# Expert passes of 112 slots instead of 128, with further passes that overlap

## The chip, the cores and the metric

The kernel runs on one core of a Trainium2 chip. The metric is the device time of one execution in microseconds (us); of several runs the median is taken. The core has five engines that work through their own instruction lists and wait for each other on semaphores: TensorE (PE, with its weight loads shown apart as PEld), VectorE (DVE), ScalarE (ACT), GpSimd (POOL) and SyncE (SP, which here only issues transfers).

## The reference

One decoder layer over 512 tokens of 1024 features in float32. The first sub-layer mixes tokens with two attention branches; the change does not touch it. The second is a mixture of 16 SwiGLU experts with a hidden width of 512:

```
logits = t @ router_w + router_b                      # t: 512 x 1024
probs  = softmax(logits)                              # 16 experts in 4 groups
g      = the group with the largest sum of its two best probabilities
experts, weights = the two best experts inside g, weights normalised
hidden = silu(t @ w_gate[e]) * (t @ w_up[e])          # for the experts chosen
y      = sum over the two experts of weight * (hidden @ w_down[e])
x      = x + gate2 * y
```

Each token goes to two experts, so an expert gets 64 tokens on average. Routed with the reference's inputs the fullest expert gets 103 and the emptiest 39.

## The kernel before, in words

The attention part and the router take the first 490 us or so. Then `expert_pass` runs over the 16 experts, each with a fixed number of slots for its tokens: 128, one per partition. If an expert has more tokens, `over` (L2010) is set, and each engine branches into further passes over all 16 experts for the tokens past the first 128. These passes are in the program but run only in that case.

Each engine has its own `stage` function that is called once per expert X, and `expert_pass` calls it for two experts at a time (b = 0 and b = 1). The order of the work is written out by hand in these functions:

- VectorE's `pick` (L2012) compares each token's position in its expert with a row 0 to 127 and writes `sel`, a bf16 table of 0 and 1, tokens by slots. It is done for two experts at once, in the stages with b = 0.
- TensorE's `slot_table` (L1082) multiplies `sel` (stationary, 128 x 128 bf16, four tiles of tokens and two experts, so eight matmuls) with `slot_t` (moving, four columns: token number and the weight in three bf16 parts). VectorE's `slot_index` (L2021) takes from it which token and which weight each slot has. An empty slot gets token 256 with weight 0.
- GpSimd's `fetch` (L619) gathers the slots' rows of 4 KB with an indirect transfer into `gx`; `scatter` (L611) adds the finished rows `ys` to the output with another.
- TensorE's `turn_rows` (L1071) turns the rows with eight transposes. ScalarE and VectorE split the result into a high and a low part, `hgT_hi` (L1509) and `hgT_lo` (L2052).
- The weights come from memory in chunks of 1 MB, six an expert. SyncE issues them up to twelve chunks ahead. ScalarE makes the high part `w_hi` (`high_e`, L1485) and VectorE the low part `w_lo` (`low_e`, L1928) of each chunk.
- `up_chunk` (L1102) and `down` (L1113) multiply with `three` (L660), three matmuls for each product of two split numbers. The slots are the stationary side, 128 x 128, and the weights the moving side, 512 columns. There are 48 such matmuls for gate and up and 24 for down in an expert.
- The hidden values are made by `silu` (L1522, L2073), turned by four transposes in `turn_hid` (L1149), and split into `hidT_hi` (L1538) and `hidT_lo` (L2092). The down product of expert X - 1 is done in the stage of expert X, between `turn_rows` and `turn_hid`.
- VectorE's `scaled` (L2034) multiplies the product with the slot's weight and a gate into `ys` (L2030).

TensorE's order in a stage, with `z` counting chunks:

```python
up_chunk(X, 0, b, z0, z)
pe.wait_ge(hg_sp, 2 * X + 2)
up_chunk(X, 1, b, z0, z + 1)
...
up_chunk(X, 2, b, z0, z + 2)
up_chunk(X, 3, b, z0, z + 3)
...
if b == 0 and more_:
    slot_table(X + 2, e + 2)
turn_rows(X + 1, 1 - b)
if not first_:
    down(X - 1, z0 + 4, z + 4)
turn_hid(X)
```

Buffers are single or double: four split chunks, twelve raw ones, two `gx`, one `ys`. The first two slot tables are made ahead of the first stage, in two groups of four matmuls; `keep_clock` (L728) puts idle matmuls around them. The last stage makes and uses `hidT` in two halves.

Of the kernel before, what the change touches and what calls it, by code (L numbers as in the profile page):

```python
# [20 lines left out]
F32R = mybir.dt.float32r  # L21
# [28 lines left out]
PASSES = S // P  # L50
# [30 lines left out]
def hybrid_layer(nc, x, c, w_ada, b_ada, norm1_g, w_in, q_norm_g, k_norm_g, rel_bias, w_o_a, w_o_b,  # L81
# [72 lines left out]
    hgT_hi = at("hgT_hi", [2, KD, P], F32R, 144)  # L154
    hgT_lo = at("hgT_lo", [2, KD, P], F32R, 152)
# [58 lines left out]
    with ExitStack() as ctx:  # L214
# [295 lines left out]
        def _(pool):  # L510
# [100 lines left out]
            def scatter(X):  # L611

                pool.wait_ge(y_sb, 2 * X + 2)
                if X:
                    pool.wait_ge(scat, 16 * X)
                pool.indirect_dma_start(out[0], bass.IndirectOffsetOnAxis(slot_tok[:, X % N_EXP:X % N_EXP + 1], 0),  # L616
                                        (ys_last if X % N_EXP == N_EXP - 1 else ys)[:, :], None, compute_op=ALU.add).then_inc(scat, 16)

            def fetch(X):  # L619

                pool.wait_ge(idx_ok, X + 1)
                if X >= 2:
# [33 lines left out]
        def _(pe):  # L656
# [414 lines left out]
            def turn_rows(X, b):  # L1071
# [4 lines left out]
                for u in range(2):  # L1076
                    for j in range(4):
                        kk = 4 * u + j
                        last = pe.transpose(ps[2 + u][:, P * j:P * j + P], gx[b][:, P * kk:P * kk + P], ident[:, :])
                    last.then_inc(hg_ps, 1)  # L1080

            def slot_table(X, e, singly=False):  # L1082
# [6 lines left out]
                for b in range(2):  # L1089
# [3 lines left out]
                    for tt in range(NT):  # L1093
                        last = pe.matmul(ps[7][:, 4 * b:4 * b + 4], sel[b][:, tt, :],
# [7 lines left out]
            def up_chunk(X, cc, b, z0, z):  # L1102
# [10 lines left out]
            def down(X, z0, z, halves=(0, 1)):  # L1113
# [16 lines left out]
            def down_last(X, z0, z, turn):  # L1130
# [4 lines left out]
                for n in range(2):  # L1135
                    for f in range(4):
# [5 lines left out]
                        m = three(ps[5 + n][:, :], (hidT_hi[:, f, :], hidT_lo[:, f, :]),  # L1142
# [65 lines left out]
        def _(act):  # L1208
# [297 lines left out]
            def hg_high(X, b):  # L1506
                for u in range(2):
                    act.wait_ge(hg_ps, 2 * X + u + 1)
                    act.activation(hgT_hi[:, b, 4 * u:4 * u + 4, :], ps[2 + u][:, :].rearrange("p (k s) -> p k s", k=4),  # L1509
                                   ACT.Copy).then_inc(hg_hi, 1)  # L1510

            def stage(X, Y, b, first_, last_):
# [9 lines left out]
                act.activation(silu[:, :], ps[0][:, :], ACT.Silu).then_inc(silu_ok, 1)  # L1522
# [7 lines left out]
                if last_:  # L1530
                    act.activation(hidT_hi[:, 0:2, :], ps[4][:, 0:2 * P].rearrange("p (k s) -> p k s", k=2), ACT.Copy
# [33 lines left out]
        def _(dve):  # L1565
# [444 lines left out]
            dve.tensor_scalar(over[:, :], over_f[:, :], P + 0.5, None, ALU.is_gt).then_inc(route_ok, 1)  # L2010

            def pick(X, e):  # L2012
# [3 lines left out]
                for b in range(2):  # L2016
                    dve.tensor_tensor(sel[b][:, :, :], iota[:, :].unsqueeze(1).broadcast_to([P, NT, P]),
                                      posm[:, :, bass.ds(e + b, 1)].broadcast_to([P, NT, P]), ALU.is_equal
                                      ).then_inc(sel_ready, 1)

            def slot_index(X, e, again, b):  # L2021
# [4 lines left out]
                dve.tensor_scalar(slot_tok[:, bass.ds(e + b, 1)], ps[7][:, 4 * b:4 * b + 1], float(S // 2), None, ALU.add)  # L2026
                dve.tensor_reduce(slot_w[:, bass.ds(e + b, 1)], ps[7][:, 4 * b + 1:4 * b + 4], AX.X, ALU.add).then_inc(idx_ok, 1)
# [122 lines left out]
```

## Time and profile before

| what | value |
|---|---|
| median of 3 runs | 819.32 us (815.22, 819.32, 819.73) |
| profiled execution: span from the first to the last instruction | 816.0 us |
| what lies around that span, if it is as long as the median run | 3.3 us |
| TensorE busy, of the span | 757.9 us (93%) |
| VectorE busy | 613.6 us (75%) |
| ScalarE busy | 430.4 us (53%) |
| GpSimd busy | 111.9 us (14%) |
| mean granted TensorE clock | 0.977 |

Times in the profile are microseconds from the start of the span. Matmuls are pipelined: a matmul's listed duration is longer than the distance to the next one, so TensorE's pace is read from the starts. A value in brackets after an instruction says how long its engine stood idle before it and which instruction ended that.

### The profile page before, as it was taken

The page shows a single profiled execution, that of the slowest core. Times are in us where ns is not written, and L with a number is a line of the kernel's source. Part 1 is how long each engine was busy: PE and PEld are TensorE (multiplying, and loading weights), DVE is VectorE, ACT ScalarE, POOL GpSimd, SP SyncE. Part 2 cuts the span into 40 slices and gives each one's busy share as a digit, 9 for nine tenths or more (in the row PEclk, how much of TensorE's full clock was granted, in tenths as well). Part 3 has the DMA queues.
Part 4 walks back from the last instruction along what each step waited for, and adds up shares of the span by engine and source line. Part 5 has one row for each costly group of instructions (what it writes and reads, how often), then busy time and mean ns, then how long its engine had stood idle before and what let it go on. Part 6 is the DMA issues. An engine that isn't in the chain of part 4 may idle for free.

```text
span 816.0 us, 9977 instructions
## 1 busy us (share of the span) xinstructions
PE 757.9 (93%) x3620; PEld 577.3 (71%) x3622; DVE 613.6 (75%) x803; ACT 430.4 (53%) x519; POOL 111.9 (14%) x90
## 2 busy tenths in 40 slices
PE   3899999999999898999999997999999999999992
PEld 3777777776665555667888874778888888788872
DVE  4676896623999958653566656799999999999991
ACT  6335124256665443555423442677767777767760
POOL 4020000000010100002000012013132232413111
PEclk9799999999999998999999999999999999999997
DMA  9928997110130131105438235999999999999973
GB/s 286 333 65 307 381 378 274 52 52 1 52 104 1 52 104 53 43 12 190 144 116 304 106 147 170 413 413 383 369 382 385 387 387 387 387 386 381 366 259 55
DMA packets 87307, 184.93 MB, mean 227 GB/s; under 512 B 8112, under 2 KB 27672, under 8 KB 85216
## 3 DMA queue, kind: packets, MB, share of 16 engines
q1 hardware_dynamic: 79200, 156.29, 51.2%
q0 software_dynamic: 8064, 28.09, 11.9%
q8 instruction: 24, 0.39, 0.2%
q14 instruction: 19, 0.16, 0.1%
HBM read 171.74 MB, written 12.62 MB: 226 GB/s over the span
## 4 chain that ended last, share of the span: by engine, by line
PE 51%; DVE 29%; issue 7%; ACT 5%; DMA 4%; SPq 1%; DVEq 1%; POOL 0%; ACTq 0%; POOLq 0%
PE ps L662 14%; PE ps L664 13%; PE ps L663 13%; DVE w_lo L1928 8%; DVE score L1750 3%; DVE ys L2030 3%; DVE m L1749 2%; ACT w_hi L1485 2%; DMA raw<-in_w_in 2%; DVE w_lo L1580 2%; PE ps L916 1%; PE ps L932 1%; DVE score L1736 1%; PE ps L944 1%; DVE sp L1701 1%
## 5 line engine op out<-in xcount | busy, mean ns | idle before, releaser
L1928 DVE TENSOR_TENSOR w_lo<-raw,w_hi 128x2048 fp32r<-128x2048 f32 x80 | 179.6, 2286 | 5.8 <-ACT w_hi L1485 5.8
L1485 ACT ACTIVATE w_hi<-raw 128x2048 fp32r<-128x2048 f32 x80 | 150.9, 1915 | 6.2 <-DMA raw<-in_w_gate 3.2
L662 PE MATMUL ps<-w_lo,hgT_hi 128*128 128x512 f32 x256 | 103.9, 406 | 4.3 <-DVE hgT_lo L2052 1.5
L662 PE MATMUL ps<-act_lo,w_hi 128*128 128x512 f32 x232 | 98.7, 426 | 5.3 <-issue 2.8
L663 PE MATMUL ps<-w_hi,hgT_lo 128*128 128x512 f32 x256 | 100.5, 393 | 0.0
L664 PE MATMUL ps<-w_hi,hgT_hi 128*128 128x512 f32 x256 | 100.5, 392 | 0.0
L664 PE MATMUL ps<-act_hi,w_hi 128*128 128x512 f32 x232 | 91.5, 395 | 0.0
L663 PE MATMUL ps<-act_hi,w_lo 128*128 128x512 f32 x232 | 91.4, 394 | 0.0
L1224 ACT ACTIVATE w_hi<-raw 128x2048 fp32r<-128x2048 f32 (+2 forms) x29 | 51.9, 1793 | 67.9 <-DMA raw<-in_w_in 44.9
L1580 DVE TENSOR_TENSOR w_lo<-raw,w_hi 128x2048 fp32r<-128x2048 f32 (+2 forms) x29 | 61.9, 2144 | 32.5 <-ACT w_hi L1224 32.3
L616 POOL DMA_INDIRECT out<-ys,slot_tok x15 | 48.8, 3255 | 159.2 <-DVE ys L2030 159.2
L662 PEld LDWEIGHTS ps<-act_lo,w_hi 128*128 128x128 f32 x232 | 44.0, 189 | 29.1 <-issue 14.6
L662 PEld LDWEIGHTS ps<-w_lo,hgT_hi 128*128 128x128 f32 x256 | 48.4, 189 | 20.5 <-DVE w_lo L1928 7.7
L664 PEld LDWEIGHTS ps<-w_hi,hgT_hi 128*128 128x128 f32 x256 | 48.5, 189 | 10.7
L663 PEld LDWEIGHTS ps<-w_hi,hgT_lo 128*128 128x128 f32 x256 | 48.6, 190 | 9.2
L662 PE MATMUL ps<-w_lo,act_hi 128*128 128x512 f32 x128 | 52.6, 411 | 1.3 <-DVE w_lo L1580 1.3
L662 PE MATMUL ps<-w_lo,hidT_hi 128*128 128x512 f32 x128 | 51.3, 401 | 2.1 <-issue 2.1
L664 PEld LDWEIGHTS ps<-act_hi,w_hi 128*128 128x128 f32 x232 | 44.0, 190 | 9.9
L664 PE MATMUL ps<-w_hi,act_hi 128*128 128x512 f32 x128 | 50.6, 395 | 0.0
L663 PE MATMUL ps<-w_hi,act_lo 128*128 128x512 f32 x128 | 50.5, 395 | 0.0
L664 PE MATMUL ps<-w_hi,hidT_hi 128*128 128x512 f32 x128 | 50.1, 391 | 0.0
L663 PE MATMUL ps<-w_hi,hidT_lo 128*128 128x512 f32 x128 | 49.9, 389 | 0.0
(279 smaller groups left out, 1378.1 us busy)
## 6 DMA issues: line engine op xcount, KB each, us to landing
raw<-in_w_down SPq DMA_DIRECT2D x32, 1024.0 KB, 16.9
raw<-in_w_gate SPq DMA_DIRECT2D x30, 1024.0 KB, 16.6
raw<-in_w_up SPq DMA_DIRECT2D x18, 1024.0 KB, 16.3
raw<-in_w_in SPq DMA_DIRECT2D x16, 1024.0 KB, 6.2
raw<-in_w_ada SPq DMA_DIRECT2D x16, 1024.0 KB, 7.3
raw_late<-in_w_up SPq DMA_DIRECT2D x14, 1024.0 KB, 19.0
raw<-in_w_ada SPq DMA_DIRECT2D x8, 512.0 KB, 6.6
raw_early<-in_w_ada SPq DMA_DIRECT2D x8, 512.0 KB, 5.5
```

The source lines that it names most:

```text
L616: pool.indirect_dma_start(out[0], bass.IndirectOffsetOnAxis(slot_tok[:, X % N_EXP:X % N_EXP + 1], 0), (ys_last if X % N_EXP == N_EXP - 1 e ...
L662: pe.matmul(o, a[0], b[1], start=start, stop=False)
L663: pe.matmul(o, a[1], b[0], start=False, stop=False)
L664: return pe.matmul(o, a[0], b[0], start=False, stop=stop)
L916: pe.matmul(zt[p % 2][:, r, 0:n], head(qbT, 2 * hp + r, P * i, P * i + P), kbT[DH * r:DH * r + DH, 0:n], start=True, stop=False, skip_grou ...
L1224: act.activation(cols(w_hi[spl_slot[w]], 0, top, nk), cols(raw[raw_slot[n]], 0, top, nk), ACT.Copy).then_inc(hi_ready, 1)
L1485: act.activation(e_hi[s_][:, :], e_raw[r][:, :], ACT.Copy).then_inc(e_top, 1)
L1580: dve.tensor_tensor(lo, r, hi.bitcast(F32), ALU.subtract).then_inc(chunk_split, 1)
L1749: link(dve.max(m8[r % 2][:, :], sc))
L1750: link(dve.match_replace(sc, m8[r % 2][:, :], sc, TAKEN))
L1928: dve.tensor_tensor(e_lo[s_][:, :], e_raw[r][:, :], e_hi[s_][:, :].bitcast(F32), ALU.subtract).then_inc(e_split, 1)
L2030: dve.scalar_tensor_tensor(out=dst[:, 512 * n:512 * n + 512], in0=ps[5 + n][:, :], scalar=slot_w[:, bass.ds(e, 1)], in1=gate2[:, 512 * n:5 ...
```

## The change

The number of slots becomes a constant, CAP = 112. All tiles with one column or row per slot shrink from 128 to 112, on the partitions or along the free dimension. The further passes become four (five passes in all), each shifted by 100 slots, so that two passes overlap by 12; the weights of tokens that an earlier pass has done are set to zero there.

```
-PASSES = S // P
+CAP = 112
+PASSES = -(-S // CAP)
+SHIFT = (S - CAP) // (PASSES - 1)
...
-    hgT_hi = at("hgT_hi", [2, KD, P], F32R, 144)
+    hgT_hi = at("hgT_hi", [2, KD, CAP], F32R, 144)
...
-    sel = [at(f"sel{i}", [NT, P], BF16, (200, 172)[i]) for i in range(2)]
+    sel = [at(f"sel{i}", [NT, CAP], BF16, (200, 172)[i]) for i in range(2)]
...
-    hidT_hi = at("hidT_hi", [4, P], F32R, 180)
+    hidT_hi = at("hidT_hi", [4, CAP], F32R, 180)
...
-                pool.indirect_dma_start(out[0], bass.IndirectOffsetOnAxis(slot_tok[:, X % N_EXP:X % N_EXP + 1], 0),
-                                        (ys_last if X % N_EXP == N_EXP - 1 else ys)[:, :], None, compute_op=ALU.add).then_inc(scat, 16)
+                pool.indirect_dma_start(out[0], bass.IndirectOffsetOnAxis(slot_tok[0:CAP, X % N_EXP:X % N_EXP + 1], 0),
+                                        (ys_last if X % N_EXP == N_EXP - 1 else ys)[0:CAP, :], None, compute_op=ALU.add).then_inc(scat, 16)
...
-                pool.indirect_dma_start(gx[X % 2][:, :], None, rows_d,
+                pool.indirect_dma_start(gx[X % 2][0:CAP, :], None, rows_d,
...
-                        last = pe.transpose(ps[2 + u][:, P * j:P * j + P], gx[b][:, P * kk:P * kk + P], ident[:, :])
+                        last = pe.transpose(ps[2 + u][:, CAP * j:CAP * j + CAP], gx[b][0:CAP, P * kk:P * kk + P],
+                                            ident[0:CAP, 0:CAP])
...
-                        last = pe.matmul(ps[7][:, 4 * b:4 * b + 4], sel[b][:, tt, :],
+                        last = pe.matmul(ps[7][0:CAP, 4 * b:4 * b + 4], sel[b][:, tt, :],
...
-                    m = three(ps[cc // 2][:, :], (hgT_hi[:, b, kk, :], hgT_lo[:, b, kk, :]),
+                    m = three(ps[cc // 2][0:CAP, :], (hgT_hi[:, b, kk, :], hgT_lo[:, b, kk, :]),
...
-                            m = three(ps[5 + n][:, :], (hidT_hi[:, f, :], hidT_lo[:, f, :]),
+                            m = three(ps[5 + n][0:CAP, :], (hidT_hi[:, f, :], hidT_lo[:, f, :]),
...
-                    t = pe.transpose(ps[4][:, P * f:P * f + P], silu[:, P * f:P * f + P], ident[:, :])
+                    t = pe.transpose(ps[4][:, CAP * f:CAP * f + CAP], silu[0:CAP, P * f:P * f + P], ident[0:CAP, 0:CAP])
...
-                act.activation(hidT_hi[:, :, :], ps[4][:, :].rearrange("p (k s) -> p k s", k=4), ACT.Copy
+                act.activation(hidT_hi[:, :, :], ps[4][:, 0:4 * CAP].rearrange("p (k s) -> p k s", k=4), ACT.Copy
...
-            dve.tensor_scalar(over[:, :], over_f[:, :], P + 0.5, None, ALU.is_gt).then_inc(route_ok, 1)
+            dve.tensor_scalar(over[:, :], over_f[:, :], CAP + 0.5, None, ALU.is_gt).then_inc(route_ok, 1)
...
-                    dve.tensor_tensor(sel[b][:, :, :], iota[:, :].unsqueeze(1).broadcast_to([P, NT, P]),
-                                      posm[:, :, bass.ds(e + b, 1)].broadcast_to([P, NT, P]), ALU.is_equal
+                    dve.tensor_tensor(sel[b][:, :, :], iota[:, 0:CAP].unsqueeze(1).broadcast_to([P, NT, CAP]),
+                                      posm[:, :, bass.ds(e + b, 1)].broadcast_to([P, NT, CAP]), ALU.is_equal
...
-                dve.scalar_tensor_tensor(out=dst[:, 512 * n:512 * n + 512], in0=ps[5 + n][:, :],
-                                         scalar=slot_w[:, bass.ds(e, 1)], in1=gate2[:, 512 * n:512 * n + 512],
+                dve.scalar_tensor_tensor(out=dst[0:CAP, 512 * n:512 * n + 512], in0=ps[5 + n][0:CAP, :],
+                                         scalar=slot_w[0:CAP, bass.ds(e, 1)], in1=gate2[0:CAP, 512 * n:512 * n + 512],
...
-                    dve.tensor_tensor(hgT_lo[:, b, 4 * u:4 * u + 4, :], ps[2 + u][:, :].rearrange("p (k s) -> p k s", k=4),
+                    dve.tensor_tensor(hgT_lo[:, b, 4 * u:4 * u + 4, :], ps[2 + u][:, 0:4 * CAP].rearrange("p (k s) -> p k s", k=4),
...
-                dve.tensor_tensor(silu[:, :], ps[1][:, :], silu[:, :], ALU.mult).then_inc(hid_ok, 1)
+                dve.tensor_tensor(silu[0:CAP, :], ps[1][0:CAP, :], silu[0:CAP, :], ALU.mult).then_inc(hid_ok, 1)
...
-                    dve.tensor_scalar(posm[:, :, :], posm[:, :, :], float(-P), None, ALU.add).then_inc(posm_ok, 1)
-                    dve.wait_ge(posm_ok, p)
+                    dve.tensor_scalar(posm[:, :, :], posm[:, :, :], float(-SHIFT), None, ALU.add).then_inc(posm_ok, 1)
+                    dve.wait_ge(posm_ok, p * 2 - 1)
+                    for n in range(1, 4):
+                        last = dve.scalar_tensor_tensor(out=slot_t[:, :, :, n], in0=posm[:, :, :], scalar=CAP - SHIFT - 0.5,
+                                                        in1=slot_t[:, :, :, n], op0=ALU.is_ge, op1=ALU.mult)
+                    last.then_inc(posm_ok, 1)
+                    dve.wait_ge(posm_ok, p * 2)
```

Left out are the same edit for hgT_lo, hidT_lo, slot_tok, slot_w, ScalarE's hgT_hi and silu, the last down product and the halves of hidT in the last stage.

## Rows read from the trace of the kernel before

**Rows 1.** Stages: start:end, length, busy us of each engine, clock, DMA share, GB/s.

```profile
500.00:520.00 20.00, 15.67 (x77) 12.49 (x76) 10.73 (x13) 7.79 (x9) 1.78 (x3) 0.91 0.91 327
640.00:680.00 40.00, 39.75 (x197) 32.33 (x196) 38.89 (x32) 27.79 (x23) 11.31 (x5) 1.00 1.05 387
```

**Rows 2.** Chain that ended last, in order of time: start, us, what.

```profile
639.33 0.50 PE ps L662
...
657.48 0.50 PE ps L662
...
675.92 0.50 PE ps L662
...
712.50 0.50 PE ps L662
```

**Rows 3.** Timeline of all engines, 640 to 661: start, us, instruction, idle before.

```profile
649.18 0.60 ACT L1538 ACTIVATE hidT_hi<-ps 128x512 fp32r<-128x512 f32 x1 [3.47 <-PE ps L1153]
...
651.52 0.39 PE L664 MATMUL ps<-w_hi,hgT_hi 128*128 128x512 f32 x1
...
651.61 2.29 DVE L1928 TENSOR_TENSOR w_lo<-raw_late,w_hi 128x2048 fp32r<-128x2048 f32 x1 [1.11 <-ACT w_hi L1485]
...
656.97 0.39 PE L664 MATMUL ps<-w_hi,hgT_hi 128*128 128x512 f32 x1
...
660.37 0.27 PEld L1094 LDWEIGHTS ps<-slot_t,sel 128*128 128x128 bf16 x8 [0.27 <-issue]
...
660.57 0.86 PEld L1079 LDWEIGHTS ps<-ident,gx 128*128 128x128 f32 x8
```

**Rows 4.** Timeline of all engines, 667 to 672.

```profile
667.61 0.60 ACT L1538 ACTIVATE hidT_hi<-ps 128x512 fp32r<-128x512 f32 x1 [3.46 <-PE ps L1153]
...
668.11 5.51 ACT L1485 ACTIVATE w_hi<-raw 128x2048 fp32r<-128x2048 f32 x3
...
669.41 0.69 DVE L2092 TENSOR_TENSOR hidT_lo<-ps,hidT_hi 128x512 fp32r<-128x512 f32 x1
...
670.05 2.29 DVE L1928 TENSOR_TENSOR w_lo<-raw,w_hi 128x2048 fp32r<-128x2048 f32 x1
```

**Rows 5.** Weight loads by form, whole span: count, then busy us, mean ns, idle.

```profile
L663 PEld LDWEIGHTS ps<-w_hi,hgT_lo 128*128 128x128 f32 x256 | 48.6, 190 | 9.2
...
L1079 PEld LDWEIGHTS ps<-ident,gx 128*128 128x128 f32 x128 | 14.3, 140 | 4.8 <-DMA gx<-rows_scratch,slot_tok 3.8
...
L944 PEld LDWEIGHTS ps<-pT,vb 128*64 128x64 f32 x80 | 5.1, 140 | 5.0 <-issue 3.3
...
L1094 PEld LDWEIGHTS ps<-slot_t,sel 128*128 128x128 bf16 x64 | 2.2, 96 | 4.6 <-DVE sel L2017 2.7 <-issue 1.8
```

**Rows 6.** Timeline of TensorE, 330 to 385: matmuls of 512 columns in bf16.

```profile
347.30 0.38 PE L922 MATMUL ps<-masks,identb 128*128 128x512 bf16 x1 [0.16 <-issue]
353.74 0.61 PE L922 MATMUL ps<-masks,identb 128*128 128x512 bf16 x2
...
366.06 0.60 PE L922 MATMUL ps<-masks,identb 128*128 128x512 bf16 x2
```

**Rows 7.** VectorE and ScalarE by form, 490 to 816.

```profile
L2092 DVE TENSOR_TENSOR hidT_lo<-ps,hidT_hi 128x512 fp32r<-128x512 f32 x15 | 10.3, 689 | 0.5 <-ACT hidT_hi L1538 0.5
L2017 DVE TENSOR_TENSOR sel<-iota,posm 128x512 bf16<-128x512 f32 x16 | 10.3, 686 | 0.0
...
L2082 DVE TENSOR_TENSOR hidT_lo<-ps,hidT_hi 128x256 fp32r<-128x256 f32 x1 | 0.4, 420 | 0.0
...
L1538 ACT ACTIVATE hidT_hi<-ps 128x512 fp32r<-128x512 f32 x15 | 9.0, 599 | 48.0 <-PE ps L1153 48.0
...
L1531 ACT ACTIVATE hidT_hi<-ps 128x256 fp32r<-128x256 f32 x1 | 0.4, 385 | 0.5 <-PE ps L1153 0.5
```

**Rows 8.** GpSimd's DMA queue, 497 to 504 (gathers) and 796 to 816 (scatters).

```profile
q0 software_dynamic: 231, 0.86, 39.7%
...
q0 software_dynamic: 288, 1.05, 34.2%
```

**Rows 9.** ScalarE's weight parts, by form and first wait for a transfer.

```profile
L1485 ACT ACTIVATE w_hi<-raw 128x2048 fp32r<-128x2048 f32 x80 | 150.9, 1915 | 6.2 <-DMA raw<-in_w_gate 3.2 <-DMA raw<-in_w_down 2.6 <-PE ps L664 0.2
...
713.16 1.92 ACT L1485 ACTIVATE w_hi<-raw 128x2048 fp32r<-128x2048 f32 x1 [0.66 <-DMA raw<-in_w_gate]
```

More of the change, by code:

```diff
@@ L153, in hybrid_layer @@
     lbias = at("lbias", [N_EXP], F32, 173.65625)
-    hgT_hi = at("hgT_hi", [2, KD, P], F32R, 144)
-    hgT_lo = at("hgT_lo", [2, KD, P], F32R, 152)
+    hgT_hi = at("hgT_hi", [2, KD, CAP], F32R, 144)
+    hgT_lo = at("hgT_lo", [2, KD, CAP], F32R, 152)
     amp2r = at("amp2r", [D], F32, 160)
@@ L161, in hybrid_layer @@
     gx = [at(f"gx{i}", [D], F32, 164 + 4 * i) for i in range(2)]
-    sel = [at(f"sel{i}", [NT, P], BF16, (200, 172)[i]) for i in range(2)]
+    sel = [at(f"sel{i}", [NT, CAP], BF16, (200, 172)[i]) for i in range(2)]
     silu = at("silu", [F_EXP], F32, 178)
-    hidT_hi = at("hidT_hi", [4, P], F32R, 180)
-    hidT_lo = at("hidT_lo", [4, P], F32R, 198)
+    hidT_hi = at("hidT_hi", [4, CAP], F32R, 180)
+    hidT_lo = at("hidT_lo", [4, CAP], F32R, 198)
     gate2 = at("gate2", [D], F32, 174)
@@ L1141, in down_last @@
                             pe.wait_ge(hidT_sp2, turn)
-                        m = three(ps[5 + n][:, :], (hidT_hi[:, f, :], hidT_lo[:, f, :]),
+                        m = three(ps[5 + n][0:CAP, :], (hidT_hi[:, f, :], hidT_lo[:, f, :]),
                                   (e_hi[s_][:, a:a + 512], e_lo[s_][:, a:a + 512]), f == 0, f == 3)
@@ L1508, in hg_high @@
                     act.wait_ge(hg_ps, 2 * X + u + 1)
-                    act.activation(hgT_hi[:, b, 4 * u:4 * u + 4, :], ps[2 + u][:, :].rearrange("p (k s) -> p k s", k=4),
+                    act.activation(hgT_hi[:, b, 4 * u:4 * u + 4, :], ps[2 + u][:, 0:4 * CAP].rearrange("p (k s) -> p k s", k=4),
                                    ACT.Copy).then_inc(hg_hi, 1)
@@ L1521, in stage @@
                     act.wait_ge(hidT_ps, X)
-                act.activation(silu[:, :], ps[0][:, :], ACT.Silu).then_inc(silu_ok, 1)
+                act.activation(silu[0:CAP, :], ps[0][0:CAP, :], ACT.Silu).then_inc(silu_ok, 1)
                 if not first_:
@@ L1530, in stage @@
                 if last_:
-                    act.activation(hidT_hi[:, 0:2, :], ps[4][:, 0:2 * P].rearrange("p (k s) -> p k s", k=2), ACT.Copy
+                    act.activation(hidT_hi[:, 0:2, :], ps[4][:, 0:2 * CAP].rearrange("p (k s) -> p k s", k=2), ACT.Copy
                                    ).then_inc(hidT_h, 1)
@@ L1534, in stage @@
                     act.wait_ge(hidT_sp, X + 1)
-                    act.activation(hidT_hi[:, 2:4, :], ps[4][:, 2 * P:4 * P].rearrange("p (k s) -> p k s", k=2), ACT.Copy
+                    act.activation(hidT_hi[:, 2:4, :], ps[4][:, 2 * CAP:4 * CAP].rearrange("p (k s) -> p k s", k=2), ACT.Copy
                                    ).then_inc(hidT_h2, 1)
                     return
-                act.activation(hidT_hi[:, :, :], ps[4][:, :].rearrange("p (k s) -> p k s", k=4), ACT.Copy
+                act.activation(hidT_hi[:, :, :], ps[4][:, 0:4 * CAP].rearrange("p (k s) -> p k s", k=4), ACT.Copy
                                ).then_inc(hidT_h, 1)
@@ L2081, in stage @@
                     dve.wait_ge(hidT_h, X + 1)
-                    dve.tensor_tensor(hidT_lo[:, 0:2, :], ps[4][:, 0:2 * P].rearrange("p (k s) -> p k s", k=2),
+                    dve.tensor_tensor(hidT_lo[:, 0:2, :], ps[4][:, 0:2 * CAP].rearrange("p (k s) -> p k s", k=2),
                                       hidT_hi[:, 0:2, :].bitcast(F32), ALU.subtract).then_inc(hidT_sp, 1)
@@ L2086, in stage @@
                     dve.wait_ge(hidT_h2, last_)
-                    dve.tensor_tensor(hidT_lo[:, 2:4, :], ps[4][:, 2 * P:4 * P].rearrange("p (k s) -> p k s", k=2),
+                    dve.tensor_tensor(hidT_lo[:, 2:4, :], ps[4][:, 2 * CAP:4 * CAP].rearrange("p (k s) -> p k s", k=2),
                                       hidT_hi[:, 2:4, :].bitcast(F32), ALU.subtract).then_inc(hidT_sp2, 1)
@@ L2091, in stage @@
                 dve.wait_ge(hidT_h, X + 1)
-                dve.tensor_tensor(hidT_lo[:, :, :], ps[4][:, :].rearrange("p (k s) -> p k s", k=4),
+                dve.tensor_tensor(hidT_lo[:, :, :], ps[4][:, 0:4 * CAP].rearrange("p (k s) -> p k s", k=4),
                                   hidT_hi[:, :, :].bitcast(F32), ALU.subtract).then_inc(hidT_sp, 1)
```

6 lines of the change are left out of this document (3 added, 3 removed).

## The prediction

> **What bounds the kernel now.** The change touches only the experts, the last 326 us or so, so I read that stretch alone. The table of stages shows the matrix engine and VectorE both nearly full in it: of 40 us PE is busy 39.75 and DVE 38.89, at full clock [rows 1]. Busy shares do not say which of the two sets the pace, so the chain of waits comes next. It repeats every two experts: a matmul that waits for a weight part opens at 639.33, 657.48, 675.92, 712.50 [rows 2]. A half without a slot table (639.33 to 657.48) takes 18.15 us, a half with one (657.48 to 675.92) 18.44, the pair 36.59; 675.92 to 712.50 is the same again.
>
> The timeline shows one loop in both halves. PE runs 12 matmuls, eight transposes of gathered rows, 24 down matmuls and four hidden transposes. ScalarE sits idle for 3.47 us until those transposes end, turns them (hidT_hi at 649.18), and only then makes the next w_hi, for which VectorE waits 1.11 us (651.61) [rows 3]. Two w_lo parts with ys between them follow, and the second releases PE at 657.48. From hidT_hi to that release it is 8.3 us. In the other half the same steps stand at 667.61, 668.11 and 670.05, and 668.11 plus one w_hi of 1.92 is 670.03: again the ACT step releases VectorE, though VectorE has only just ended hidT_lo (669.41 plus 0.69) [rows 4]. So what counts is what lies in PE's part of the loop (about 9.8 us, 10.1 with a slot table), hidT_hi, w_hi, two w_lo and ys. Other VectorE work counts only once it is late.
>
> **The change, part by part.**
>
> *Further passes.* The fullest expert holds 103 tokens (worked out by routing the reference's inputs). 103 is under 112 as it is under 128, the branch is not taken, and the new code in it (three multiplies a pass, a fifth pass) costs nothing. Were it taken, four more passes of some 300 us each would stand in the time.
>
> *The matmuls of the experts.* The moving side stays 512 wide; the slots are the stationary side, whose load shrinks from 128 to 112 columns. Loads get cheaper by the column: 128 columns take 190 ns, 64 take 140 [rows 5], 0.78 ns a column, so 112 should show some 177. But PE does not wait for a load: 24 steps from 651.52 to 656.97 give a pitch of 0.227 us [rows 3], of which 512 columns at 2.4 GHz are 0.213, and the load lies under it. What the other 0.014 us is, decides. If it is a fixed price of changing weights, 112 columns save nothing; if it follows the columns, an eighth of it, 1.7 ns; if the load's whole shortening came back, 13 ns. In the loop are 36 matmuls an expert, so 16 experts give 0, 1.0 or 7.7 us. The nearest row is a bf16 pair of 512 columns: alone 0.38, as a pair 0.60 to 0.61, a pitch of 0.22 to 0.23 [rows 6], though its loads take half as long (rows below). A load half as long leaves the pitch as it was, so I take a fixed price: 0. The range keeps 7.7.
>
> *The slot table's loads.* This is the part against the change. These matmuls take sel as bf16 stationary, and sel goes from 128 to 112 columns. I take the slow way at 112 columns, 0.103 x 112 / 128 = 0.090, because nothing in the rows shows the fast way for anything but 128 columns. A table of eight then costs 8 x (0.090 - 0.025) = 0.52 us more. PE works in order, and behind the table wait the row transposes, the down matmuls and the hidden transposes, hence ScalarE, VectorE and the end of the half: it is inside the loop. There are 64 such loads [rows 5]: the opening two groups of four, one table in the first stage, six in the steady halves. Seven tables are 3.6 us; of the opening 0.52 I count 0.4, the first group running beside the second sel. Sum +4.0.
>
> The Trainium skill, page "TensorE: Matmul & The Clock Gate", section "Weight-path perf modes — Fast Weight Load (FWL) and DoubleRow", has this as a rule: the fast load is on only when the number of weights is 128 and the type is not FP32. The trace agrees for full loads (bf16 fast, f32 slow); no row shows a narrower bf16 load. By that rule the sum below stands; without it, it is 4.0 lower. The section "LDWEIGHTS (loading the stationary operand)" there puts a load at columns / 1.2, by which I estimate 93 ns for 112 columns, much as the slow slope does.
>
> *Evictions and picks by the slot.* hidT, hgT and sel have 448 elements a partition instead of 512. hidT_lo takes 689 ns for 512 and 420 for 256, so 64 fewer save 0.067; hidT_hi 599 and 385, so 0.053; sel (686) counts as hidT_lo [rows 7]. In the loop only hidT_hi is on the path: 16 x 0.053 = 0.85. In the run-up two sel, three hgT_hi and one hgT_lo give 0.35. The rest falls into VectorE's slack and is worth nothing unless PE gets faster. If VectorE's tie at 670.05 were binding, it would give up to 0.33 a pair, but the later slot table takes its place. Sum -1.2. silu and ys lose partitions, not elements: 0, for want of a row that shows a gain.
>
> *Rows fetched and scattered.* Sixteen of 128 descriptors fall away. On the path are the first gather (PE has nothing before it) and the last scatter. Two scatters keep the DMA engines busy 34.2% of 20 us, 3.4 us each; gathers 39.7% of 7 us for 231 packets, 1.5 us per 128 [rows 8]. An eighth of each: 0.43 and 0.19. The issue of the first gather may shrink too, or not: 0 to 0.3. Taken: -0.6. The 14 gathers and 15 scatters between are hidden.
>
> *Transposes.* Their stationary side stays 128 columns (the model dimension); rows and moving columns become 112. The load sets their pitch: 0. Bound above: a rival.
>
> **Sum.** +4.0 - 1.2 - 0.6 + 0 = +2.2 us on the profiled span of 816.0, so 818.2. The median of the runs, 819.32, lies 3.3 above that span; I keep this difference: 821.5 us. The three runs are 4.5 us apart, so under 0.5% (4.1 us) cannot be told from no change.
>
> **Rivals.** *The fast bf16 load survives 112 columns.* Then -1.8, 817.5 us. For it: the load is still most of the array. Against it: no row. Chance 0.25.
>
> *The weight load does space the stream.* The 0.014 us falls with the columns: by an eighth, 820.5; altogether, 813.8, and PE leaves the loop's 9.8 us by 0.48 a half. For it: all f32r rows pay it. Against it: the bf16 pair. Chance 0.08 for the eighth, 0.07 for all.
>
> *Slower: the f32 transposes lose their short load.* They load 140 ns where plain f32 takes 190 [rows 5]. If 112 rows bar them from that, each of 12 an expert costs 50 ns more, 0.6 us a half inside PE's part, 9.6 in all: 831. It decides from 20 ns a transpose on, beside the tables. Against it: columns, not rows, set load times in the trace. Chance 0.05. Also on this side: the clock. Between 500 and 520 the mean granted clock was 0.91 [rows 1], so part of that stretch ran at 1.2 GHz, 0.09 x 20 = 1.8 us lost, after PE had idled for the first rows; slower opening tables shift that, and a second such stretch would bring 823.3.
>
> *The transfers set the pace.* ScalarE waits for weights from 713.16 on, 5.8 us in all [rows 9]; fewer row descriptors would take that away: down to 815.7. Against it: the pair's length is the same before the first wait (639.33 to 675.92) and at 675.92 to 712.50, and ScalarE has idle time each half. Chance 0.08.
>
> *The change does not do what it says* (further passes run): 0.01.
>
> **Chances and range.** The forecast has 0.46. It ends slower by over 0.5% in 0.10 of that, the transposes and the clock add 0.09, unforeseen waits 0.03: slower 0.22. Faster: the whole of the pitch 0.07, transfers 0.05, a part of the surviving fast load 0.05, the rest 0.02: 0.19. Within 0.5%: 0.59. The range runs from the transfers' case with a little more, 815.0, to the forecast with a second slow-clock stretch and a dearer load (0.103), 825.0; left out are the whole pitch below and the transposes above.
>
> **What would show it.** Right: the slot table's loads at some 170 ns instead of 96, about 0.09 apart; f32r pitch still 0.227; hidT_hi near 546 ns; the pair near 37.0 us, its half with the table longer by 0.47 and the other shorter by 0.05. Wrong: loads at 96 (the pair 36.5), a pitch near 0.215, transposes' loads at 190, or ScalarE's waits for weights gone together with a shorter pair.

## The result and the profile after

| what | before | after |
|---|---|---|
| median of 4 runs each, on one chip | 819.53 us | 826.99 us (825.03 to 829.73) |
| ratio after to before, 95% interval | | 1.0124 [1.0093, 1.0155] |
| profiled execution: span | 816.0 us | 822.9 us (its run: 825.03 us) |
| first to fifteenth scatter | 250.86 us | 261.82 us |

The change costs 1.2%. The prediction was 821.5 us with a range up to 825.0, so it was too low. Times of kernels with the fault found below spread by up to 2%: runs more than 1.5% above the fastest of their kernel are left out of the ratios, and three of their profiles (e6, e7, f2) are of such long executions.

The page of after says where to look. GpSimd was busy for 111.9 us before; now the scatter alone takes 144.4, and the chain that ended last lies for a quarter of the span on the scatter's transfer (DMA 4% of it before).

```profile
PE 759.5 (92%) x3622; PEld 560.5 (68%) x3622; DVE 611.2 (74%) x803; ACT 428.3 (52%) x519; POOL 202.3 (25%) x90
...
DMA out<-ys,slot_tok 25%; PE ps L664 10%; PE ps L666 9%; PE ps L665 9%; DVE score L1753 3%; DVE m L1752 3%; DMA raw<-in_w_ada 2%; DVE w_lo L1583 2%; DVE ys L2033 1%; PE ps L918 1%; DVE score L1739 1%; DVE sp L1704 1%; PE ps L934 1%; DVE w_lo L1931 1%; DVE accm L1642 1%
...
L618 POOL DMA_INDIRECT out<-ys,slot_tok x15 | 144.4, 9627 | 121.9 <-DVE ys L2033 121.9
```

By stages, what [rows 1] showed is less full: PE and DVE lost some 2.4 and 1.5 us of 40, GpSimd more than doubled. (The clock from 500 to 520 is 1.00 here.)

```profile
500.00:520.00 20.00, 17.34 (x90) 13.05 (x91) 13.81 (x17) 12.06 (x12) 1.84 (x2) 1.00 0.98 364
640.00:680.00 40.00, 37.33 (x180) 27.98 (x179) 37.42 (x32) 27.48 (x22) 26.09 (x5) 1.00 1.04 367
```

The chain over one pair answers to [rows 2]. It no longer goes through PE: scatter, landing, ys, scatter.

```profile
638.76 0.75 DVE ys L2033
639.51 0.27 issue
639.78 16.48 DMA out<-ys,slot_tok
...
658.07 17.65 DMA out<-ys,slot_tok
...
676.51 0.75 DVE ys L2033
677.26 0.27 issue
677.53 16.54 DMA out<-ys,slot_tok
```

There is one buffer ys, so `scaled` (L2037) waits until the scatter before it has landed. Landing 16.48, then 1.81 to the next scatter (two halves of ys 1.41, the gaps before and behind them 0.40) make 18.29, the distance from 639.78 to 658.07; 17.65 + 1.81 = 19.46, the distance to 677.53. That is the pair of 37.75 us, 36.59 before. Before, the scatter at 637.35 landed after 10.9 us, and the next ys began at 653.82, 16.5 us after its start: 5.6 us to spare.

The timeline of VectorE and GpSimd in the same half shows why the landing is late. The scatter begins 0.36 us into the first of four w_lo and ends 1.47 us after silu begins. The last scatter, with VectorE idle, takes 1.47 us in all.

```profile
639.42 8.89 DVE L1931 TENSOR_TENSOR w_lo<-raw,w_hi 128x2048 fp32r<-128x2048 f32 x4
639.78 9.91 POOL L618 DMA_INDIRECT out<-ys,slot_tok  x1 [5.48 <-DVE ys L2033]
648.22 0.68 DVE L2076 TENSOR_TENSOR silu<-ps,silu 112x512 f32<-112x512 f32 x1
...
811.32 1.47 POOL L618 DMA_INDIRECT out<-ys_last,slot_tok  x1 [6.78 <-DVE ys_last L2033]
```

The lines of the kernel before in such a half:

```profile
636.99 8.89 DVE L1928 TENSOR_TENSOR w_lo<-raw,w_hi 128x2048 fp32r<-128x2048 f32 x4
637.35 3.39 POOL L616 DMA_INDIRECT out<-ys,slot_tok  x1 [3.57 <-DVE ys L2030]
...
653.82 1.40 DVE L2030 SCALAR_TENSOR_TENSOR ys<-ps,slot_w,gate 128x512 f32<-128x512 f32 x2
```

A scatter's length and end are what the profile gives; that it waits first and works in its last 1.47 us is read from these ends. So GpSimd waits for 8.4 us, through w_lo after w_lo (two inputs from SBUF each), and works when silu (one input from PSUM) begins. Before, the same scatter took 3.4 us: it ended 1.5 us after the first boundary between two w_lo (639.19), and ran beside the second w_lo without making it longer. Both start 0.36 us after their w_lo does. What changed is that it no longer gets in at a boundary.

The Trainium skill, page "SBUF — State Buffer", section "Who interferes with whom", says that VectorE and GpSimd share one pair of SBUF ports as a lock and that a VectorE instruction with two SBUF inputs contends with a GpSimd instruction that reads SBUF. The long waits agree; the scatters before, which ran beside a w_lo, do not fit a plain lock.

The rows that answer to [rows 5], [rows 7] and [rows 9], by form (ScalarE waits for weights 1.2 us at most now, being held up itself):

```profile
L665 PEld LDWEIGHTS ps<-w_hi,hgT_lo 128*112 128x112 f32 x256 | 45.1, 176 | 13.3
L1081 PEld LDWEIGHTS ps<-ident,gx 112*128 112x128 f32 x128 | 13.6, 144 | 3.8 <-DMA gx<-rows_scratch,slot_tok 2.5 <-issue 0.2
L1097 PEld LDWEIGHTS ps<-slot_t,sel 128*112 128x112 bf16 x64 | 4.5, 131 | 3.4 <-DVE sel L2020 2.3
...
L1541 ACT ACTIVATE hidT_hi<-ps 128x448 fp32r<-128x448 f32 x15 | 8.2, 545 | 49.6 <-PE ps L1156 49.6
...
L1488 ACT ACTIVATE w_hi<-raw 128x2048 fp32r<-128x2048 f32 x79 | 149.5, 1914 | 2.8 <-PE ps L666 1.6
...
L2033 DVE SCALAR_TENSOR_TENSOR ys<-ps,slot_w,gate 112x512 f32<-112x512 f32 x30 | 21.1, 746 | 8.9 <-DMA out<-ys,slot_tok 7.1 <-PE ps L666 1.8
```

### The profile page after: what moved, and what is told of

Its sections match the earlier page's. It is cut to its first block, busy times and chain, and to the rows that moved or that the text cites. A ratio compares the mean times of both kernels' runs of the same rounds, so it can differ in the third digit from the quotient of the medians.

```text
span 822.9 us, 9979 instructions
## 1 busy us (share of the span) xinstructions
PE 759.5 (92%) x3622; PEld 560.5 (68%) x3622; DVE 611.2 (74%) x803; ACT 428.3 (52%) x519; POOL 202.3 (25%) x90
## 3 DMA queue, kind: packets, MB, share of 16 engines
q0 software_dynamic: 7552, 25.99, 11.5%
## 4 chain that ended last, share of the span: by engine, by line
PE 39%; DMA 29%; DVE 19%; issue 7%; ACT 4%; SPq 1%; POOL 1%; DVEq 0%; POOLq 0%; ACTq 0%
DMA out<-ys,slot_tok 25%; PE ps L664 10%; PE ps L666 9%; PE ps L665 9%; DVE score L1753 3%; DVE m L1752 3%; DMA raw<-in_w_ada 2%; DVE w_lo L1583 2%; DVE ys L2033 1%; PE ps L918 1%; DVE score L1739 1%; DVE sp L1704 1%; PE ps L934 1%; DVE w_lo L1931 1%; DVE accm L1642 1%
## 5 line engine op out<-in xcount | busy, mean ns | idle before, releaser
L618 POOL DMA_INDIRECT out<-ys,slot_tok x15 | 144.4, 9627 | 121.9 <-DVE ys L2033 121.9
L664 PE MATMUL ps<-w_lo,hgT_hi 128*112 128x512 f32 x256 | 103.9, 406 | 11.3 <-DVE w_lo L1931 9.8
L666 PE MATMUL ps<-w_hi,hgT_hi 128*112 128x512 f32 x256 | 101.9, 398 | 0.0
L665 PE MATMUL ps<-w_hi,hgT_lo 128*112 128x512 f32 x256 | 100.9, 394 | 0.0
L664 PEld LDWEIGHTS ps<-w_lo,hgT_hi 128*112 128x112 f32 x256 | 44.8, 175 | 31.0 <-DVE w_lo L1931 14.9
L666 PEld LDWEIGHTS ps<-w_hi,hgT_hi 128*112 128x112 f32 x256 | 44.8, 175 | 14.8
L664 PE MATMUL ps<-w_lo,hidT_hi 128*112 128x512 f32 x128 | 52.1, 407 | 2.6 <-issue 2.6
L665 PEld LDWEIGHTS ps<-w_hi,hgT_lo 128*112 128x112 f32 x256 | 45.1, 176 | 13.3
L666 PE MATMUL ps<-w_hi,hidT_hi 128*112 128x512 f32 x128 | 51.3, 401 | 0.0
L665 PE MATMUL ps<-w_hi,hidT_lo 128*112 128x512 f32 x128 | 50.8, 397 | 0.0
```

The costliest lines, as they stand in the source:

```text
L664: pe.matmul(o, a[0], b[1], start=start, stop=False)
L665: pe.matmul(o, a[1], b[0], start=False, stop=False)
L666: return pe.matmul(o, a[0], b[0], start=False, stop=stop)
```

## The experiments

In each, "issue" is the time of one scatter on GpSimd (median of 15), and the ratio is to the kernel before on the same chip.

**First: is it the 112-row scatter?** e1 is the kernel before with this alone, e4 the same with 96; e2 is the changed kernel with sel, slot table, index, ys and scatter back at 128; e3 the changed kernel with one more instruction in each stage.

```diff
-  ...slot_tok[:, X % N_EXP:...], (ys_last if ... else ys)[:, :]
+  ...slot_tok[0:112, X % N_EXP:...], (ys_last if ... else ys)[0:112, :]      # e1; 0:96 in e4
```

```diff
                 low_e(z + 3, z0 + 3)
+                if not first_ and not second_:                                # e3
+                    dve.tensor_copy(qkg[:, 0:64], ps[7][:, 64:128])
```

> The kernel before, in which the scatter alone takes 112 rows (slots 112 to 127, all empty here, are not added); slot tables, picks, gathers, transposes, matmuls and evictions keep 128 slots. Theory (the loss is the scatter's: with 112 rows its issue on GpSimd no longer gets in between two of VectorE's instructions, and ys waits for it): GpSimd's scatter lengthens from 3.3 us to 9 to 10 us in the mean, its landing from 10.9 to some 16.5 us, VectorE's ys waits 5 to 7 us in all for it, pairs of 37.5 us or more instead of 36.6, time 5 to 8 us over the kernel before (824 to 828). Rival (the loss sits in TensorE's part, from the slower loads of the slot table and the f32r pitch of 0.231): scatter still 3.3 us, time within 1.5 us of the kernel before.

> The kernel before, in which the scatter alone takes 96 rows; the tokens of slots 96 and up (seven, all of the one fullest expert) are not added to the output. Theory A (any number of rows that is not 128 makes the issue miss the gap between two VectorE instructions): issue 9 us or more, time as with 112 rows, 824 to 828. Theory B (a multiple of 32 rows still gets in): issue 2.7 to 3.4 us, time that of the kernel before or 1 us less. Rival (the loss is not the scatter's at all): issue 3.3 us or a little less, no change.

> The changed kernel with sel, the slot table, its index and weight, ys and the scatter back at 128 slots; the gather, the transposes, silu, hgT, hidT and all f32r matmuls stay at 112. Theory (scatter): the scatter's issue falls back to 3.3 to 3.6 us, its landing to some 11 us, ys waits for nothing but TensorE; time 818 to 821, that is, the kernel before's less the shorter evictions (0.85) or with the longer pitch (0.003 us x 36 x 16 = 1.7) added. Rival (TensorE's part): what is left in it, the f32r pitch of 0.231, carries most of the loss, and the time stays at 823 or more. Read beside it: the f32r pitch at 112 stationary columns, 0.231 again if the columns set it, 0.228 if it came with the scatter.

> The changed kernel with one more VectorE instruction in each steady stage: a copy of 64 columns from PSUM into a spare SBUF buffer (a dead value) after the second of the low parts w_lo, so that VectorE's run of subtractions that read two SBUF inputs is broken by an instruction that reads none. Theory (the 112-row scatter waits on GpSimd through the whole run of such subtractions and starts when it ends): the scatter's issue drops from 9.6 us to 5 or less, the wait of ys shrinks to under 2 us in all, and 4 to 7 us come back (819 to 823). Rival (112 rows take GpSimd longer to work through, whatever VectorE does): the issue stays at 9 to 10 us and the time is that of the changed kernel or longer by the copies, 827 to 829.

| run | ratio | issue, us | landing, us |
|---|---|---|---|
| e1 | 0.9989 [0.9969, 1.0010] | 3.29 | 10.4 |
| e4 | 0.9971 [0.9947, 0.9995] | 3.25 | 9.5 |
| e2 | 1.0029 [1.0012, 1.0046] | 3.36 | 10.4 |
| e3 | 0.9980 [0.9959, 1.0002] | 3.30 | 10.3 |

The row count is not the cause: my first theory fell (e1 and e4 came out as its rivals had it). That it is the scatter stands: e3 takes the whole loss back with 14 copies of 0.22 us, and in its timeline the scatter gets in at the copy (635.62 + 1.47 = 637.09, its end).

```profile
633.42 2.28 DVE L1931 TENSOR_TENSOR w_lo<-raw,w_hi 128x2048 fp32r<-128x2048 f32 x1
635.62 0.22 DVE L2066 COPY qkg<-ps 128x64 f32<-128x64 f32 x1
635.76 6.68 DVE L1931 TENSOR_TENSOR w_lo<-raw,w_hi 128x2048 fp32r<-128x2048 f32 x3
...
633.78 3.31 POOL L618 DMA_INDIRECT out<-ys,slot_tok  x1 [3.79 <-DVE ys L2033]
```

**Second: which of the narrowed parts?** e5 is the changed kernel with ys on 128 partitions; e6 the kernel before with ys and scatter at 112; e7 the changed kernel with pick, table and index at 128; e8 the kernel before with all narrowed but the f32r matmuls, their transposes, evictions and silu.

```diff
-  dve.scalar_tensor_tensor(out=dst[0:CAP, ...], in0=ps[5 + n][0:CAP, :],      # e5; the reverse in e6
-                           scalar=slot_w[0:CAP, ...], in1=gate2[0:CAP, ...],
+  dve.scalar_tensor_tensor(out=dst[:, ...], in0=ps[5 + n][:, :],
+                           scalar=slot_w[:, ...], in1=gate2[:, ...],
```

> The changed kernel with ys alone written on all 128 partitions again (the slot weights past 112 are zero); pick, slot table, index, gather, scatter and matmuls stay at 112. The runs so far say that neither the scatter's 112 rows alone nor the gathers, transposes and f32r matmuls of 112 starve the scatter; left are ys on 112 partitions and the pick with its slot table, alone or together with the scatter. Theory Y (ys on 112 partitions is needed): scatter's issue 3.3 us, time 815 to 819. Rival T (the narrower pick and slot table do it): issue 9 to 10 us as in the changed kernel, time 825 to 829.

> The kernel before with ys and the scatter at 112 partitions and rows, all else at 128 (slots 112 to 127 are empty). Theory Y (ys on 112 partitions, read by a scatter of 112 rows, is enough by itself): issue 9 us or more, time 823 to 828. Rival T: issue 3.3 us, time that of the kernel before, 816 to 820.

> The changed kernel with sel, the slot table's matmuls, the token index and the weight back at 128 slots; gather, matmuls, ys and scatter stay at 112. Theory T (the narrower pick is needed for the starving): issue 3.3 us, time 815 to 820, and pairs of some 36.3 us, 0.2 shorter than in the run with the copy, whose tables are still slow. Theory Y: issue 9 to 10 us, time 823 to 828.

> The kernel before with pick, slot table, index, gather, ys and scatter at 112, and the f32r matmuls, their transposes and evictions and silu at 128: the changed kernel without the smaller stationary side. If the stationary side has no part in the starving (theories Y and T alike): issue 9 to 10 us, time 824 to 829. Rival (the starving needs the changed timing of TensorE or ScalarE too): issue 3.3 us, time 817 to 821, the longer slot tables (0.17 us each) in it.

| run | ratio | issue, us | landing, us |
|---|---|---|---|
| e5 | 1.0006 [0.9983, 1.0028] | 3.30 | 10.3 |
| e6 | 1.0174 [1.0089, 1.0258] | 9.92 | 17.0 |
| e7 | 1.0096 [1.0066, 1.0125] | 9.91 | 17.1 |
| e8 | 1.0150 [1.0078, 1.0222] | 9.91 | 17.1 |

Theory Y holds in all four for the issue; the times of e6 and e8 (833.6 and 832.8 us) lie above what was expected. e1 and e6 differ only in the partition count of ys, an instruction that takes the same 0.74 us and ends the same 0.28 us before the scatter; the issue goes from 3.29 to 9.92 us.

```profile
L616 POOL DMA_INDIRECT out<-ys,slot_tok x15: 1462/3292/3337, 545.5 to 796.5; - x15
```

```profile
L616 POOL DMA_INDIRECT out<-ys,slot_tok x15: 1462/9915/11147, 547.0 to 819.2; - x15
```

(The scatter's line in e1, then in e6: ns, minimum, median and maximum.)

**Third: ys itself, the last instruction, or any partial one?** A copy of 64 elements stands behind ys: full in the changed kernel (e9), on 112 partitions in the kernel before (e10), full in the kernel before (f1). In f3 the copy on 112 stands in front of ys. e11 has ys and scatter at 96, f2 only the first half of ys at 112.

```diff
+  dve.tensor_copy(qkg[0:112, 0:64], ps[7][0:112, 64:128])                     # f3
   scaled(X - 2, e - 2, b)
+  dve.tensor_copy(qkg[:, 0:64], ps[7][:, 64:128])                             # e9, f1; 0:112 in e10
```

```diff
+  rows = 112 if n == 0 else P                                                 # f2
+  dve.scalar_tensor_tensor(out=dst[0:rows, ...], in0=ps[5 + n][0:rows, :], ...
```

> The changed kernel (ys on 112 partitions) with a copy of 128 partitions x 64 elements from PSUM into a spare SBUF buffer directly behind ys, so that it has ended before the scatter starts; the run of w_lo behind it is unbroken. Theory L (what counts is the partition count of VectorE's last instruction before the run of full ones): scatter's issue 3.1 to 3.4 us, time 815 to 820. Rival D (what counts is that the rows of ys itself were written on 112 partitions): issue 9 to 11 us, time 823 or more.

> The kernel before (ys and scatter at 128) with a copy of 112 partitions x 64 elements from PSUM into a spare SBUF buffer directly behind ys. Theory L (the last instruction before the run): the 128-row scatter starves too, issue 9 to 11 us, time 823 or more. Rival D (ys itself): issue 3.1 to 3.4 us, time 816 to 820.

> The kernel before with ys and scatter at 96 partitions and rows (the seven tokens of the fullest expert in slots 96 and up are not added to the output). Theory P (anything less than 128 partitions starves the scatter): issue 9 to 11 us, time 823 or more. Rival Q (only a number that is no multiple of 32 does, and 96 does not): issue 3.1 to 3.4 us, time 815 to 819.

> The kernel before with a full copy (128 partitions x 64 elements, PSUM to a spare SBUF buffer) directly behind ys: the control of the run with the copy on 112 partitions. Theory S (a VectorE instruction on fewer than 128 partitions shortly before the run makes the scatter miss its boundaries, and a full one does not undo it): with no partial instruction there the issue stays at 3.1 to 3.5 us and the time at 817 to 821, the copies' 0.13 us a half in it. Rival M (it is the extra 0.13 us, which moves the boundary from 1.84 to 1.97 us behind the scatter's start, or the copy as such): issue 9 to 11 us, time 830 or more.

> The kernel before with the scatter at 112 rows and only the first of the two instructions of ys on 112 partitions, the second on 128; nothing added, so every boundary stays where it was. Theory S (a partial instruction shortly before, not undone by a full one behind it): issue 9 to 11 us, time 823 or more. Rival L (only the last instruction before the run counts): issue 3.3 us, time 816 to 820.

> The kernel before with the copy on 112 partitions x 64 elements placed in front of the two full instructions of ys instead of behind them. Theory S: the scatter starves as it does with the copy behind ys, issue 9 to 11 us, time 823 or more. Rival L (only the last instruction before the run counts): issue 3.3 us, time 817 to 821.

| run | partial instruction | ratio | issue, us |
|---|---|---|---|
| e9 | ys, then a full copy | 1.0178 [1.0135, 1.0220] | 10.04 |
| e10 | copy behind a full ys | 1.0338 [1.0296, 1.0381] | 10.13 |
| e11 | ys at 96 | 1.0145 [1.0103, 1.0187] | 9.87 |
| f1 | none | 1.0023 [0.9997, 1.0049] | 3.51 |
| f2 | first half of ys | 1.0183 [1.0111, 1.0255] | 9.92 |
| f3 | copy in front of a full ys | 1.0316 [1.0276, 1.0357] | 3.4 and 11.2 in turn |

e9 and e10 each refuted one of their two theories: it is neither the last instruction alone (e9) nor ys (e10, where a scatter of all 128 rows starves). f1 clears the copy. What is common to all starved kernels is a VectorE instruction on fewer than 128 partitions shortly before the run, and a full one behind it does not undo that. 96 is no better than 112; one scatter of e11, the fourteenth, was worse and let silu (one input from PSUM) pass as well:

```profile
792.24 12.97 POOL L616 DMA_INDIRECT out<-ys,slot_tok  x1 [8.29 <-DVE ys L2030]
```

f3 came out as neither of its theories had it, and shows the exception. Where copy and ys follow each other the scatter starves; where VectorE stood idle for 1.85 us between them, it does not:

```profile
604.41 0.22 DVE L2060 COPY qkg<-ps 112x64 f32<-112x64 f32 x1
606.48 1.41 DVE L2030 SCALAR_TENSOR_TENSOR ys<-ps,slot_w,gate 128x512 f32<-128x512 f32 x2 [1.85 <-DMA out<-ys,slot_tok]
...
608.17 3.39 POOL L616 DMA_INDIRECT out<-ys,slot_tok  x1 [5.67 <-DVE ys L2030]
...
626.22 0.22 DVE L2060 COPY qkg<-ps 112x64 f32<-112x64 f32 x1
626.35 1.40 DVE L2030 SCALAR_TENSOR_TENSOR ys<-ps,slot_w,gate 128x512 f32<-128x512 f32 x2
...
628.03 11.17 POOL L616 DMA_INDIRECT out<-ys,slot_tok  x1 [16.46 <-DVE ys L2030]
```

**Fourth: is it the idle time?** f4 puts the copy in front of the last w_lo of a stage.

```diff
+  if not first_:
+      dve.tensor_copy(qkg[0:112, 0:64], ps[7][0:112, 64:128])
   low_e(nz + 2, nz0 + 2)
```

> The kernel before with the copy on 112 partitions x 64 elements one instruction earlier still: in front of the last w_lo of each stage, so that copy, w_lo, ys, ys follow each other and then the run. In the run before this one (copy in front of ys) the scatters alternated: 11.2 us where copy and ys followed without a gap, 3.4 us where VectorE stood idle for 2.6 us between them. Theory I (an idle VectorE between the partial instruction and the run undoes it, busy time does not): in the stages with b = 1, whose last w_lo waits about 1.1 us for w_hi, the next scatter issues in 3.3 to 3.5 us; in the stages with b = 0, where it follows at once, the next scatter takes 9.9 us; once ys is late in them, as in the other runs. Rival W (a full instruction with two SBUF inputs undoes it): all at 3.3 to 3.5 us, time 817 to 821. Rival N (nothing does but the scatter's getting in): all at 9.9 to 11.3 us, time 830 or more.

The ratio is 1.0052 [1.0030, 1.0073], and the scatters alternate as theory I has it: 10.0 us where copy, w_lo and ys follow each other, 3.4 us where w_lo waits.

```profile
632.34 0.21 DVE L2095 COPY qkg<-ps 112x64 f32<-112x64 f32 x1
632.47 2.28 DVE L1928 TENSOR_TENSOR w_lo<-raw,w_hi 128x2048 fp32r<-128x2048 f32 x1
...
649.42 0.21 DVE L2095 COPY qkg<-ps 112x64 f32<-112x64 f32 x1
650.61 2.29 DVE L1928 TENSOR_TENSOR w_lo<-raw_late,w_hi 128x2048 fp32r<-128x2048 f32 x1 [0.98 <-ACT w_hi L1485]
...
636.35 9.99 POOL L616 DMA_INDIRECT out<-ys,slot_tok  x1 [3.69 <-DVE ys L2030]
655.21 3.38 POOL L616 DMA_INDIRECT out<-ys,slot_tok  x1 [8.86 <-DVE ys L2030]
```

Rival W falls: a full w_lo stands between copy and run in both halves, although the time alone (819.85 us) is inside what W had. Nor is it only the time that has passed: in f3 above the copy ended 3.54 us before the scatter that gets in, here 3.80 us before one that starves. In between lay 1.85 us of idle time there, none here.

Idle time is enough, then, but not always needed. silu and the slot index run on 112 partitions in e5 and do no harm, with 0.30 us or more of idle VectorE behind them; but in the same halves of e2 VectorE idles for 0.01 us at most, in those of e12 (the last version, below) not at all, and the scatter still gets in. The lines of e12, where VectorE has no idle time from silu to the scatter:

```profile
622.16 0.68 DVE L2076 TENSOR_TENSOR silu<-ps,silu 112x512 f32<-112x512 f32 x1
...
626.29 0.62 DVE L2095 TENSOR_TENSOR hidT_lo<-ps,hidT_hi 128x448 fp32r<-128x448 f32 x1
626.85 2.29 DVE L1931 TENSOR_TENSOR w_lo<-raw,w_hi 128x2048 fp32r<-128x2048 f32 x1
629.06 1.40 DVE L2033 SCALAR_TENSOR_TENSOR ys<-ps,slot_w,gate 128x512 f32<-128x512 f32 x2
...
630.74 3.31 POOL L618 DMA_INDIRECT out<-ys,slot_tok  x1 [3.55 <-DVE ys L2033]
```

Between them lie 7.9 us, several full instructions that read PSUM, and a gather in which GpSimd itself worked. No run tells which of these undid it.

**Last: a version from what was learnt.** e12 narrows rows (gather, scatter, transposes, evictions) and keeps 128 where a stationary side or ys is meant.

```diff
-    hgT_hi = at("hgT_hi", [2, KD, CAP], F32R, 144)                            # hgT_lo, hidT, sel alike
+    hgT_hi = at("hgT_hi", [2, KD, P], F32R, 144)
-                    m = three(ps[cc // 2][0:CAP, :], (hgT_hi[:, b, kk, :], hgT_lo[:, b, kk, :]),
+                    m = three(ps[cc // 2][:, :], (hgT_hi[:, b, kk, :], hgT_lo[:, b, kk, :]),
```

> A version put together from the runs: gather, row and hidden transposes, evictions and scatter at 112, but sel, slot table, index, ys and the stationary side of the f32r matmuls on 128 (columns 112 to 127 of hgT and hidT zeroed once). By the rows it should keep the pitch at 0.228 instead of 0.232 (72 x 0.0034 = 0.25 us a half against the changed kernel without the starving), the fast loads (0.2 us a table) and the shorter transposes: halves of 17.8 and 18.0, pairs of 35.8 against 36.6. Theory (TensorE's stream is what bounds the loop once the scatter gets in): 7 pairs x 0.75 = 5 us off, 811 to 814. Rival (transfers of the weights then set the pace, as in the last 130 us of the run with the scatter at 128): ScalarE waits 15 us or more for weights and the time stays at 815 to 820.

815.23 us, ratio 0.9970 [0.9950, 0.9990]: faster than both kernels, by about half of what the first theory expected. The time and the waits are those of the rival; the theory has a part: pairs are 36.2 us up to 667 (it had 35.8), then ScalarE waits, 26.3 us in all before its w_hi and 23.4 of it for weights, and pairs grow to 38. From there on the transfers set the pace. The length of the pairs alone does not decide that: e3 has pairs of 36.5 us like e5, but ScalarE waits 13.7 us for raw weights in it and 1.7 in e5.

```profile
L1488 ACT ACTIVATE w_hi<-raw 128x2048 fp32r<-128x2048 f32 x79 | 149.9, 1916 | 26.3 <-DMA raw<-in_w_down 12.2 <-DMA raw<-in_w_gate 11.2 <-PE ps L666 2.6
```

The chain of e5, then of e12, prices the stationary side, from the first of 24 down matmuls to the hidden transposes: 5.56 us with 112 columns, 5.46 with 128.

```profile
642.48 0.77 PE ps L1081 x8
643.25 0.23 PE ps L664
...
648.81 0.39 PE ps L1156 x4
```

```profile
635.78 0.77 PE ps L1081 x8
636.55 0.24 PE ps L664
...
642.01 0.40 PE ps L1156 x4
```

## Why the prediction was wrong

*Rows fetched and scattered* is the step that failed: "The 14 gathers and 15 scatters between are hidden." The gathers are; the scatters were hidden with 5.6 us to spare and lost them. The prediction priced what a scatter moves, and silu and ys at 0 "for want of a row that shows a gain", which is right for their own time (0.746 against 0.744 us). It did not ask what an instruction on VectorE does to one on GpSimd, though the trace of before had a sign of it: the same scatter takes 3.4 us in the loop and 1.54 at the end (ns, minimum, median and maximum):

```profile
L616 POOL DMA_INDIRECT out<-ys,slot_tok x15: 1538/3376/3404, 545.8 to 796.7; - x15
```

That 112 partitions would make this three times as long, no row of before could show. What the runs showed in place of a hidden scatter: an issue of 9.91 us instead of 3.38 and a landing of 16.5 instead of 10.9, which ys waits for. e5 against after is the price: 250.29 us from first to fifteenth scatter against 261.82, so 11.5 us, of which a run-up shorter by 4.7 hides some in this profile (run-ups end between 540.1 and 547.7 in all profiles). By the ratios of the runs, 1.0006 and 1.0124, it is some 9.7 us.

With ys full, the rest of the sum would have been inside its range: e5 is at 1.0006, the forecast was +2.2 us or 1.0027. That is in part luck, for its terms were less good than their sum:

- *Further passes*: right, none ran.
- *The slot table's loads*: mis-sized. They got slower, as predicted, but to 131 ns and not 170; a table's eight matmuls take 0.53 us instead of 0.35. So 0.18 a table and 1.4 in all, not 4.0. The Trainium skill's rule (page "TensorE: Matmul & The Clock Gate", section "Weight-path perf modes — Fast Weight Load (FWL) and DoubleRow") says that the fast load is off below 128 weights. The direction agrees. The rule has no size; 131 ns lies between the full load of 96 [rows 5] and the 170 of the slope, and the measurement decides.
- *The matmuls*: a fixed price was taken, with bounds on the side of a gain alone. It is a loss: 0.2317 against 0.2275 us a step (the two chains above), and over all steps of the experts the means are 0.2317 in e5 and 0.2283 before. 72 steps make 0.25 to 0.30 us a half. Without the starving the chain of a pair of e5 goes through PE alone, so there this counts. Giving it back is worth less: steady pairs, from scatter to scatter, take 36.32 us in e2, with 112 stationary columns, and 36.19 in e12, with 128 and otherwise alike but for the rows of the scatter. In e12's chain ScalarE, VectorE and, later, the transfers set the pace again.
- *Transposes*: "0" was wrong in our favour. Their loads stayed (144 ns), but eight take 0.77 us where the chain of before has 0.87, and four 0.39 instead of 0.45: 0.16 a half.
- *Evictions*: right, hidT_hi 545 ns for 546.
- Of the rivals, *the transfers set the pace* is true only of some kernels without the fault (e12, and the late pairs of e2 and e3), and against its sign: ScalarE's waits for weights grew from 5.8 us before to 23.4 in e12, with fewer row descriptors. In after ScalarE waits for hardly any weights, because the scatter is slower than they are.

Open: how the chip decides that GpSimd misses a boundary after a partial instruction, and what ends that besides idle time (e2, e12); only where it happens was tried. Open too is why starved pairs differ between kernels (37.7 us in after, some 41 in e10, whose granted clock is 0.964), and why the weights came late in the profile of e2 (its longest run), whose median is 3 us over its kernel before although its scatters are in time.

## What to carry to other kernels

A transfer that GpSimd issues beside a busy VectorE has a slack; read it (time free less time to landing) before calling it hidden. Keep VectorE's instructions on all 128 partitions just ahead of where such a transfer is issued among instructions with two SBUF inputs, even if rows are computed for nothing, or put one instruction that reads PSUM alone into the run. And shrink moving columns and rows rather than the stationary side: 112 stationary columns made f32r matmuls and bf16 loads slower.

## What the runs showed of the hardware

- GpSimd's scatter of 1.47 us, by its end, starts at a boundary between two VectorE instructions of two SBUF inputs and runs beside the second one, which keeps its 2.28 us (e1, e5).
- Shortly after a VectorE instruction on 112 or 96 partitions it misses every such boundary of the run, three or five of them, some 8.4 or 9.6 us (e6, e8, e10, e11, f2). One small instruction of the run that reads PSUM alone lets it in (e3); 0.98 us of idle VectorE before the run do too (f4), a full copy, ys or w_lo in between does not (e9, f3, f4). After a silu on 112 partitions 7.9 us earlier it gets in without any idle time (e12); why is open.
- f32r matmuls of 512 moving columns step at 0.2317 us with 112 stationary columns, 0.2275 with 128.
- bf16 weight loads of 112 columns take 131 ns, of 128 columns 96 [rows 5].
